# A gate projection in seven block products per pair of column tiles, with half of the weight differences made by GpSimd

## The reference, cut to what matters

```
xn     = rmsnorm(x)
proj   = xn @ w_in                          # q, k, v, ssm input, memory query, and 3072 gate columns
gates  = sigmoid(proj[..., GATE_COL:])      # 3 branches x 1024
merged = gates[0] * (att @ w_att_out) + gates[1] * (ssm @ w_ssm_out) + gates[2] * (mem @ w_mem_out)
h      = x + merged @ w_o
h      = h + hier_moe(rmsnorm(h))           # 32 experts, each with three 1024 x 512 weights
```

## Time and profile before

| | |
|---|---|
| time, median of 3 runs | 1201.76 us (1199.83 to 1201.8) |
| span of the profiled execution | 1199.0 us |
| end of the last gate product, from the span's start | about 510 us |
| TensorE matmul busy | 1086.0 us, 91% |
| VectorE, ScalarE, GpSimd busy | 353.6, 232.3, 134.8 us |
| gate matmuls (L856) | 768 records, 173.1 us |

### The profile page before, as it was taken

How to read it: one execution, slowest core, us unless ns; L and a number is a source line. 1 busy time by engine, 2 the same in 40 slices (tenths; PEclk the granted TensorE clock), 3 DMA queues, 4 the chain that set the end, 5 groups by cost and what they waited for, 6 DMA issues and landing times.

```text
span 1199.0 us, 16688 instructions
## 1 busy us (share of the span) xinstructions
PE 1086.0 (91%) x6915; PEld 778.2 (65%) x6915; DVE 353.6 (29%) x761; ACT 232.3 (19%) x444; POOL 134.8 (11%) x152
## 2 busy tenths in 40 slices
PE   7999999999999999999999879997777788888875
PEld 6888888897888888878855545554444444444441
DVE  3994306923223242231544421010000000000003
ACT  4103021135222222250021211111111111110114
POOL 2113310002000100000000010111111111111010
PEclk9999999999999999999999979999899989999899
DMA  6771367324755654377347389999999999999984
GB/s 226 252 256 54 102 222 237 122 93 153 243 194 197 219 186 170 137 246 302 160 182 277 138 346 403 416 417 419 417 420 419 422 423 421 421 420 420 419 322 147
DMA packets 48938, 330.89 MB, mean 276 GB/s; under 512 B 8860, under 2 KB 12012, under 8 KB 35424
## 3 DMA queue, kind: packets, MB, share of 16 engines
q1 hardware_dynamic: 31744, 257.65, 54.0%
q0 software_dynamic: 15104, 64.44, 15.7%
q10 hardware_dynamic: 2016, 7.76, 1.6%
HBM read 319.77 MB, written 62.11 MB: 318 GB/s over the span
## 4 chain that ended last, share of the span: by engine, by line
PE 66%; DMA 29%; ACT 2%; issue 1%; SPq 1%; DVE 1%; POOLq 0%; ACTq 0%; DVEq 0%
DMA arena<-in_w 25%; PE bank L856 14%; PE bank L679 14%; PE bank L1178 8%; PE bank L1041 5%; PE bank L1203 4%; PE bank L1032 4%; PE bank L952 2%; PE bank L692 1%; PE bank L771 1%; PE bank L845 1%; DMA arena<-in_w_stream 1%; PE bank L871 1%; PE bank L892 1%; ACT arena L1450 1%
## 5 line engine op out<-in xcount | busy, mean ns | idle before, releaser
L1178 PE MATMUL bank<-arena 128*64 128x256 f32 x2048 | 262.4, 413 | 65.5 <-DMA arena<-in_w 64.9
L1178 PEld LDWEIGHTS bank<-arena 128*64 128x64 f32 x2048 | 160.3, 144 | 159.7 <-issue 58.5
L856 PE MATMUL bank<-arena 128*128 128x260 f32 x768 | 173.1, 384 | 0.0
L679 PE MATMUL bank<-arena 128*128 128x260 f32 x768 | 169.9, 383 | 0.0
L679 PEld LDWEIGHTS bank<-arena 128*128 128x128 f32 x768 | 145.4, 190 | 23.0 <-issue 0.5
L856 PEld LDWEIGHTS bank<-arena 128*128 128x128 f32 x768 | 144.1, 190 | 22.4 <-issue 1.2
L1203 PE MATMUL bank<-arena 128*64 128x512 f32 x512 | 115.6, 593 | 3.5 <-DVE arena L2039 3.5
L2033 DVE TENSOR_TENSOR arena<-arena,bank 128x256 f32<-128x256 f32 x32 | 13.5, 422 | 326.5 <-ACT arena L1507 326.5
L635 POOL DMA_INDIRECT y_dram<-arena,scatter_rows x31 | 44.3, 1430 | 384.1 <-ACT arena L1523 350.0
L1203 PEld LDWEIGHTS bank<-arena 128*64 128x64 f32 x512 | 36.7, 136 | 63.4 <-issue 54.4
L1507 ACT ACTIVATE arena<-bank 128x256 f32<-128x256 f32 x32 | 12.3, 384 | 320.5 <-PE bank L1178 320.5
(11 more groups left out here) (341 smaller groups left out, 1083.2 us busy)
## 6 DMA issues: line engine op xcount, KB each, us to landing
arena<-in_w SPq DMA_DIRECT2D x95, 2048.0 KB, 35.9
arena<-in_w_stream SPq DMA_DIRECT2D x56, 512.0 KB, 3.5
out_sample_swa_k<-in_cache_swa_k POOLq DMA_DIRECT2D x8, 2047.0 KB, 10.5
out_sample_swa_v<-in_cache_swa_v POOLq DMA_DIRECT2D x8, 2047.0 KB, 10.2
arena<-in_cache_mem_v SPq DMA_DIRECT2D x8, 512.0 KB, 6.4
arena<-in_w_o SPq DMA_DIRECT2D x2, 2048.0 KB, 15.4
out_sample_swa_k<-in_cache_swa_k POOLq DMA_DIRECT2D x8, 511.0 KB, 6.7
out_sample_swa_v<-in_cache_swa_v POOLq DMA_DIRECT2D x8, 511.0 KB, 6.2
```

Source lines behind the costliest of these rows:

```text
L679: last = pe.matmul(bank[:, 2 * u + h, 0:HALF], ring[u][:, k, :], x[:, k, h * HALF:(h + 1) * HALF], start=k == 0, stop=k == KT - 1)
L856: last = pe.matmul(bank[:, h, 0:HALF], ring[n % 2][:, k, :], xn[:, k, h * HALF:(h + 1) * HALF], start=k == 0, stop=k == KT - 1)
L1178: last = pe.matmul(bank[64 * q:64 * q + CAP, 2 + u, part * FE // 2:(part + 1) * FE // 2], xgT[e // 2 % 2][:, k, 64 * u:64 * u + CAP], w[:, ...
```

## The change

Two tiles of gate columns, 2i and 2i+1, are taken together as one product of a 2 x 2 block matrix of weights (b11, b21 the upper and lower 512 rows of tile 2i; b12, b22 of tile 2i+1) with a 2 x 2 block matrix of xn (x11, x12, x21, x22: the first number is the half of the tokens, the second the half of the rows). Seven block products replace eight; each is 4 matmuls of 128 x 128 by 260:

- sums of xn, once, on VectorE, 4 x 260 elements a row each: sum1 = x21 + x22, sum2 = sum1 - x11, sum4 = x12 - sum2, sum3 = x11 - x21 (in place of x21);
- differences of weights, for each pair, 512 elements a row each: on GpSimd t3 = b22 - b12 and t1 = b12 - b11 (`raw_terms`); on VectorE t2 = b22 - t1 (`terms`) and t4 = b21 - t2 (`last_term`);
- products: M1 = b11 x11, M6 = t2 sum2, M5 = t1 sum1, M7 = t3 sum3 in the first step, M2 = b21 x12, M3 = b22 sum4, M4 = t4 x22 in the second. M1 and M2 share bank 0, M6, M7 and M4 bank 1, M5 and M3 bank 7, each adding to what is there;
- taking out: ScalarE copies M1 (`first_product`) and M1 + M2 (`gate_out`), 260 wide; VectorE makes five sums of 260 from PSUM: `gate_v` (M1 + M6, must lie before M7), `gate_c22` (two), `gate_c12`, `gate_c21`.

Weights come as quarters of 256 KB, four for a pair, into eight rotating places. GpSimd's loop over the shift becomes a program written out over the pairs: differences of pair i, one shift part after M1 of pair i, one after M2 of pair i, and only then the differences of pair i+1. The rest follows from room: `w_ssm` is loaded by SyncE, in four pieces, only after the last product; `dist0` is stored shorter; `kv_dec`, `dpv` and the key slots move; the key and value rows are made by 12 matmuls instead of 12 transposes; two loads of `w_o` wait longer.

The diff, cut to its core:

```diff
+            for i in range(1, N_PAIR):                      # SyncE
+                done = PRODUCTS * (i - 1)
...
+                sp.wait_ge(*later("product", done + M1 + 1))
+                sp.wait_ge(*later("term", TERMS * (i - 1) + 1))
+                load_quarter(i, "b11")
+                load_quarter(i, "b12")
+                sp.wait_ge(*later("product", done + M6 + 1))
+                sp.wait_ge(*later("term", TERMS * i))
+                load_quarter(i, "b22")
+                sp.wait_ge(*later("product", done + M2 + 1))
+                load_quarter(i, "b21")
+            sp.wait_ge(*later("product", PRODUCTS * N_PAIR))
+            for k in range(4):
+                sp.dma_start(w_ssm[k], t["w_ssm"][:, k, :]).then_inc(s["wssm"], 16)
...
-            sp.wait_ge(s["dvdone"], MH * (NB - 1))
+            sp.wait_ge(s["dvdone"], MH * NB)
             sp.dma_start(w_o[1], t["w_o"][:, 4:8, :]).then_inc(s["wo"], 16)
-            sp.wait_ge(s["dvdone"], MH * NB)
+            sp.wait_ge(s["Sj"], KT)
             sp.dma_start(w_o[0], t["w_o"][:, 0:4, :]).then_inc(s["wo"], 16)
...
-            shift_caches(4, NB, N_FIRST + 1)
+            def raw_terms(i):                               # GpSimd
+                w = wq[i]
+                for name in ("b12", "b22", "b11"):
+                    pool.wait_ge(*later(name, 16 * (i + 1)))
+                if i:
+                    pool.wait_ge(*later("product", PRODUCTS * (i - 1) + M5 + 1))
+                    pool.wait_ge(*later("term", TERMS * (i - 1) + 1))
+                pool.tensor_tensor(w["t3"], w["b22"], w["b12"], ALU.subtract).then_inc(later_sem("raw_term"), 1)
+                pool.wait_ge(*later("raw_term", 2 * i + 1))
+                pool.tensor_tensor(w["t1"], w["b12"], w["b11"], ALU.subtract).then_inc(later_sem("raw_term"), 1)
...
+            for n in range(2 * N_PAIR):
+                i, second = divmod(n, 2)
+                if not second:
+                    raw_terms(i)
+                if n < 16:
+                    pool.wait_ge(*later("product", PRODUCTS * i + (FIRST_HALF if second else 0) + 1))
+                    shift_part(n)
...
+            def product(i, m):                              # TensorE
+                opens = m in (M1, M6, M5)
+                for k in range(4):
+                    last = pe.matmul(bank[:, product_bank[m], 0:HALF], wq[i][left[m]][:, k, :], right[m][:, k, :],
+                                     start=opens and k == 0, stop=k == 3, skip_group_check=True)
+                last.then_inc(later_sem("product"), 1)
+            def gate_step(n):
+                i, second = divmod(n, 2)
+                parts = 5 * i
+                if not second:
+                    pe.wait_ge(*later("b11", 16 * (i + 1)))
+                    wait_from(pe, s["gevac"], 2 * i)
+                    product(i, M1)
+                    pe.wait_ge(*later("term", TERMS * i + 1))
+                    wait_from(pe, *later("gpart", parts))
+                    product(i, M6)
+                    product(i, M5)
+                    pe.wait_ge(*later("gpart", parts + 1))
+                    product(i, M7)
+                else:
+                    pe.wait_ge(*later("b21", 16 * (i + 1)))
+                    pe.wait_ge(s["gevac"], 2 * i + 1)
+                    product(i, M2)
+                    pe.wait_ge(*later("b22", 16 * (i + 1)))
+                    pe.wait_ge(*later("gpart", parts + 3))
+                    product(i, M3)
+                    pe.wait_ge(*later("term", TERMS * (i + 1)))
+                    product(i, M4)
...
                     TS(prob[odd], prob[odd], rd, None, ALU.mult).then_inc(s["pn"], 1)   # VectorE, attention
+                    if odd == 0:
+                        gate_v(pair)
+                last_term(pair)
+                gate_c22(pair)
+                terms(pair + 1)
+                gate_c12(pair)
+                gate_c21(pair)
...
                 TS(pm[b], pm[b], rd, None, ALU.mult).then_inc(s["mpn"], 1)              # VectorE, memory
+                i = NPAIR + it // 4
+                if it % 4 == 1:
+                    gate_v(i)
+                    last_term(i)
+                    gate_c22(i)
+                if it % 4 == 3:
+                    if i + 1 < N_PAIR:
+                        terms(i + 1)
+                    gate_c12(i)
+                    gate_c21(i)
```

More of the change, by code:

```diff
@@ L78 @@
 N_FIRST = N_PROJ + N_MEMT
+QUARTER = D // 2
+N_PAIR = N_GATE // 2
+PRODUCTS = 7
+TERMS = 2
+FIRST_HALF = 4
+M1, M6, M5, M7, M2, M3, M4 = range(PRODUCTS)
 KB = 256
@@ L234, in build @@
         pmT = [at(MK + 4, MEM), at(MK + 5, MEM)]
-        slot = [(PROJ + 16 + 7 * i, PROJ + 19 + 7 * i) for i in range(4)] + [(MK, MK + 12)]
+        slot = [(PROJ + 8.25, PROJ + 11.25), (PROJ + 20.5, PROJ + 23.5), (PROJ + 32.75, PROJ + 35.75),
+                (PROJ, work + 2), (MK, MK + 12)]
         slot_k = [at(x, NG, 2, P) for x, _ in slot]
@@ L250, in build @@
         dpn = at(MK + 17, NG, 64)
-        dpv = at(work, NG, 64 * NB)
+        dpv = [at(x, 64 * NB) for x in (work, S5 + 91, MK + 6)]
         dmpv = at(PROJ + 45, 2, MH, 32 * NB)
         do_rows, dmo_rows = at(S5 + 59, P), at(work + 6, P)
-        w_att, w_ssm, w_mem = at(RING, 2, D), at(PROJ, 4, D), at(XN, 4, D)
+        w_att, w_mem = at(RING, 2, D), at(XN, 4, D)
+        w_ssm = [at(PROJ + (T_QKV + 6 * g + 4) * TOK / KB, D) for g in range(NG)] + [at(PROJ + 4, D)]
         w_o = [at(HOMES[6], 4, D), at(HOMES[8], 4, D)]
@@ L335, in h_back_in @@
                 (kdec[T], 32 * len(range(T, NB, NSLOT)) + 16)
[L337 removed]
+        late = dict(raw_term=("ucomb", CH + 3), product=("cplx", 2), term=("toep", CH), gpart=("sprev", 3), xsum=("uscaled", 1),
+                    b11=("x0", 16), b12=("x1", 16), b21=("x2", 16), b22=("x3", 16), pick=("Sfree", KT), turned=("Sj", KT), placed=("merged", KT), sums=("Pj", 2 * KT),
                     added=("Pfree", 2 * KT))
@@ L847, in _ @@
                     last.then_inc(s["job"], 1)
[L849 to L858, removed]
+            def product(i, m):
+                opens = m in (M1, M6, M5)
+                closes = m in (M2, M3, M4)
+                for k in range(4):
[24 more added lines that the diff above has]
+                    product(i, M4)
             def scores(pair):
@@ new lines, in terms, with last_term @@
+            def terms(i):
+                w = wq[i]
+                dve.wait_ge(*later("raw_term", 2 * i + 2))
+                if i:
+                    dve.wait_ge(*later("product", PRODUCTS * (i - 1) + M7 + 1))
+                TT(w["t2"], w["b22"], w["t1"], ALU.subtract).then_inc(later_sem("term"), 1)
+            def last_term(i):
+                w = wq[i]
+                dve.wait_ge(*later("b21", 16 * (i + 1)))
+                if i:
+                    dve.wait_ge(*later("product", PRODUCTS * (i - 1) + M3 + 1))
+                dve.wait_ge(*later("term", TERMS * i + 1))
+                TT(w["t4"], w["b21"], w["t2"], ALU.subtract).then_inc(later_sem("term"), 1)
@@ new lines, in gate_v, with gate_c22 @@
+            def gate_v(i):
+                dve.wait_ge(s["gevac"], 2 * i + 1)
+                dve.wait_ge(*later("product", PRODUCTS * i + M6 + 1))
+                TT(v_tmp, s1_tmp, bank[:, product_bank[M6], 0:HALF], ALU.add).then_inc(later_sem("gpart"), 1)
+            def gate_c22(i):
+                dve.wait_ge(*later("product", PRODUCTS * i + M7 + 1))
+                TT(w_tmp, s1_tmp, bank[:, product_bank[M7], 0:HALF], ALU.add).then_inc(later_sem("gpart"), 1)
+                dve.wait_ge(*later("gpart", 5 * i + 2))
+                TT(gates[:, 2 * i + 1, HALF:TOK], w_tmp, bank[:, product_bank[M5], 0:HALF], ALU.add
+                   ).then_inc(later_sem("gpart"), 1)
@@ new lines, in gate_c12, with gate_c21 @@
+            def gate_c12(i):
+                dve.wait_ge(*later("product", PRODUCTS * i + M3 + 1))
+                TT(gates[:, 2 * i + 1, 0:HALF], v_tmp, bank[:, product_bank[M3], 0:HALF], ALU.add
+                   ).then_inc(later_sem("gpart"), 1)
+            def gate_c21(i):
+                dve.wait_ge(*later("product", PRODUCTS * i + M4 + 1))
+                TT(gates[:, 2 * i, HALF:TOK], s1_tmp, bank[:, product_bank[M4], 0:HALF], ALU.add
+                   ).then_inc(later_sem("gpart"), 1)
@@ L1743, in _ @@
+            dve.wait_ge(s["yadd"], 4)
+            terms(0)
             for ct in range(4):
```

171 lines of the change are left out of this document (122 added, 49 removed).

## The result

The changed kernel takes 1194.3 us (median of four runs, 1193.6 to 1196.0) against 1201.0 us of the kernel before beside it: a ratio of 0.9947, interval 0.9932 to 0.9961. That is 6.7 us faster; the forecast was 1182.0 us, and the time lies above its range. The profiled execution has a span of 1192.9 us, 6.1 us under the 1199.0 of before, where 19.8 were forecast.

What follows compares the result with a forecast made beforehand. TensorE was taken to bound the gate stages; -21.3 + 0 + 0.6 + 0.7 + 0.2 = -19.8 us gave a span of 1179.2 us, and 2.8 us between span and timed median gave 1182.0 us. Range 1178.5 to 1191 us.

Steps and rivals of the forecast that it cites:

- the 0 that the sum has: Gate stages: the differences and sums added on VectorE and GpSimd were to cost 0 us of the span.
- TensorE sets the pace, 8 records are 1.78 us, and groups of 8 cost nothing: Gate tiles: TensorE alone bounds them; dropping 8 records for each of 12 pairs saves 21.3 us, with no grouping cost.
- The rest keeps its length: Later stage with full DMA engines: it starts earlier and keeps its length, so gate savings count at full value.
- The walk through the attention round: One attention round walked without stalls: 16.72 us instead of 18.50; M7 has 0.85 us to spare for gate_v.
- GpSimd's difference: One 512-element subtraction on GpSimd, G, taken as 1.0 us; no row showed its price.
- The notice a: GpSimd's delay in noticing M2 within an attention round: 0.15 us as other engines, up to 1.03 as before.
- the loop: Attention round through GpSimd, VectorE and TensorE: 13.68 + a + 2G, taken as 16.7 us against TensorE's 16.72.
- Rival 1: Attention rounds: GpSimd differences of 1.2 to 1.9 us hold the loop back, 2.7 to 12.5 us, 1185 to 1195 us; chance 0.16.
- Rival 2: Attention rounds: VectorE holds up GpSimd's differences, 3 us each, making the kernel slower, 1210 us; chance 0.09.
- w_ssm: Ahead of ssm_out: the load requested after the last product costs 0.3 to 1.7 us, taken as 0.7.
- rival 3: w_ssm or another late load costs 4 us, 1186 us; sign a gap over 2 us ahead of ssm_out(0); chance 0.07.

Runs made afterwards that it cites:

- the exchange of the parts: Changed kernel with the two small parts of the attention stage's cache copy sent after M1 and the 2 MB part after M2: 0.9855 of before, 1184.1 us.
- The version with both edits: Changed kernel with small cache-copy parts after M1, the 2 MB part after M2, and w_ssm requested early, after the last M5 and M3: 0.9836 of before, 1182.1 us.
- the run with the small parts: Changed kernel with the attention stage's 2 MB cache-copy parts moving a sixteenth of their bytes, same instructions, the rest left out: 0.9842 of before, 1183.8 us.
- the run with everything on VectorE: Changed kernel with t3 and t1 also made by VectorE, GpSimd only issuing the cache copy: 0.9909 of before, 1189.0 us.

## Why the prediction was wrong

The direction and the saving were right; what failed is the 0 that the sum has for the added work on VectorE and GpSimd. 6.1 us of span were gained, not 19.8. From the profiled executions, the 13.7 us that are missing are
- 7.6 us: the long rounds. From the first scores to the end of the gates the changed kernel has 210.0 us, the exchange of the parts 202.4. Three long rounds take 1.84, 1.84 and 1.51 us more than the short ones; the fourth, whose M7 waits 1.63 us, 2.1; and the wait at the change of stages behind it is 0.82 us, against 0.51 with the parts exchanged and in the kernel before;
- 2.5 us: the first round and the first pair of the memory stage. The version with both edits has no late b22, and still its 202.4 us are 18.8 less than the 221.2 of before, not 21.3;
- 2.5 us: `ssm_out(1)` comes 17.19 - 13.95 = 3.2 us later after the gates, 0.7 taken; the half clock is 1.7 of it (5.46 - 3.77);
- 0.7 us: first scores at 290.71 instead of 289.38, 0.6 of these 1.3 us taken. The same program had them at 288.50 in its other execution, so this can't be told from nothing;
- 0.3 us later, and rounding.

The step from span to time is a small error of its own: the forecast put 2.8 us between them, and in every profiled execution whose own time is on record it is 1.5 to 1.7 us (1194.48 and 1192.9 here).

Step by step:
- **TensorE sets the pace, 8 records are 1.78 us, and groups of 8 cost nothing.** Right: short rounds take 16.75 us, computed 16.72, and two memory rounds 16.67, computed 16.6.
- **The rest keeps its length.** Right: from `ssm_out(1)` to the end it is 674.5 us before and 675.0 after.
- **The walk through the attention round.** This step failed, and with it the term 0. It followed TensorE, VectorE and GpSimd, and for GpSimd it began at the copies behind M2; it left out SyncE, which asks for b22 behind t4. The landing of "some 3.5 us" was used in the memory stage alone, where no 2 MB part runs. In the attention stage every b22 stands behind one and lands only when it has landed; it comes too late whenever TensorE has not lost time in the round just before. From the part at 294.54 to t3 12.8 us, differences 2.6, t2 and sums 1.3, bias to the end of `gate_v` 5.6: 294.54 + 12.8 + 2.6 + 1.3 + 5.6 = 316.8. M7 was due at 306.78 + 8.31 = 315.1, so 1.7 us are missing, and the trace has 1.58. The part's own time stood on the page; what was missing was the question what lies ahead of a new load.
- **GpSimd's difference.** Taken 1.0, measured 1.27 us. By the page of the Trainium skill that the prediction names (GPSIMD Engine Reference, section Elementwise — side-by-side cycle accounting) a quarter of its figure was 1.12, an estimate that is nearer and still too low. The notice a is 322.23 - (320.01 + 1.78) = 0.44 us, so the loop is 13.68 + 0.44 + 2.54 = 16.66 us, still under 16.72, and the run with the small parts, which has the same copies and differences in its loop, shows it: no stall. Two errors cancelled, the price too low and a = 1.03 too high; that this left 0 was luck. But the loop had no slack left for b22, and so the price did matter, as the run with everything on VectorE shows. Rival 1 named the right narrow place and the wrong reason: its band (1185 to 1195) holds the measured time and its sign, TensorE's gap ahead of M7, showed, but with the measured price and a its own sum gives nothing.
- **Rival 2, the lock between GpSimd and VectorE.** It did not decide. It exists: see below.
- **The places that weren't walked.** In the first round M7 waits 0.52 us for `gate_v`. At the change of stages VectorE clears tiles for 2.5 us, and the first memory pair's `gate_v` comes 1.2 us late; before, a gate tile of 7.11 us lay over it. VectorE and then TensorE in the run with the parts exchanged:

```profile
425.26 1.34 DVE L1972 MEMSET arena<- 128x1536 f32 x1 [0.27 <-issue]
426.76 1.12 DVE L1972 MEMSET arena<- 128x1024 f32 x2 [0.16 <-issue]
```

```profile
432.70 2.02 PE L957 MATMUL bank<-arena 128*128 128x260 f32 x8 [1.20 <-DVE arena L1906]
```

  That the clearing is what delays it is read from the order of VectorE; no run moved it. The change also takes the memory values of two heads out in one copy instead of two (`mo_copy`), which the list of the change leaves out; no run parts this from the rest.
- **w_ssm, and rival 3.** 15.26 - 13.95 = 1.3 us where the clock stays up: inside 0.3 to 1.7, 0.7 taken; 3.2 us in the execution with the half clock. The gap of over 2 us ahead of `ssm_out(0)`, rival 3's sign, showed (2.42 and 2.16), at a smaller price than its 4 us. But rival 3 said "`w_ssm` or another late load", and a late load it was: b22, 7.6 us, for which the prediction gave no place and no walk.

## What to carry to other kernels

A new wait on a loaded operand is walked back to the load's request, and then to what is queued or running on the DMA engines at that moment; a landing time from a quiet stretch does not hold behind a copy of 2 MB. Of two copies that have two places to go, the larger goes behind the request of the load that is wanted next: one exchanged line brought 7.6 us in the trace here (210.0 to 202.4 from the first scores to the end of the gates), and 0.9 points of the ratio. And where an engine's new work has just enough time by the sum, a late input comes through: GpSimd's 2.2 to 2.9 us of standing ahead of t3 came out as 1.25 to 1.63 us of TensorE's wait ahead of M7.

## What the runs showed of the hardware

- A load of 256 KB asked for 5 us behind a copy of 2 MB from DRAM to DRAM was there for t3 only 7.7 us later, when the copy was done; the median of such loads in that stretch is 4.0 us. All eight b22 of the changed kernel landed 0.2 to 1.0 us after the copy ahead of them (9.6 to 12.3 us long). Of the sixteen loads of b11 and b12 that were asked for within 0.3 us of a copy's issue, fourteen landed after 2.7 to 4.1 us, and two after 8.3 and 11.0. Whether b22 queued behind the copy's packets or shared the engines with them no run tells.
- A subtraction of 128x512 in SBUF takes GpSimd 1.27 us and VectorE 0.69 us, both in f32.
- VectorE's division of 128x256 took 1.34 us instead of 0.35 when it began while GpSimd subtracted. In the run with the parts exchanged, VectorE above and GpSimd below:

```profile
437.48 1.34 DVE L2000 TENSOR_SCALAR arena<-arena 128x256 f32<-128x256 f32 x1
440.18 0.35 DVE L2000 TENSOR_SCALAR arena<-arena 128x256 f32<-128x256 f32 x1
```

```profile
437.41 1.27 POOL L676 TENSOR_TENSOR arena<-arena 128x512 f32<-128x512 f32 x1
```

  The first ends as GpSimd's does, 438.8 and 438.7. The Trainium skill (SBUF — State Buffer, section Who interferes with whom) says that the two share a pair of ports, which one instruction holds to its end; this trace agrees. Here it costs nothing, as TensorE had work.
- After about 2 us of idle TensorE ahead of `ssm_out(0)` the granted clock fell to 0.50 in one execution (2.42 us idle) and not in the other of the same program (2.16 us), nor in the five other versions with such a wait (2.09 to 2.27 us).
